# Where the last two slots of the input projection are computed in a two-block decoder kernel

## The reference

```
for l in range(2):
    h = x @ w_in[l]                  # gla: q k v g lr | rwkv: r k v w a g | nsa: q kc vc ks vs kw vw gate
    o_gla  = gla_mixer(q, k, v, g, lr)              # chunked decayed linear attention
    o_rwkv = rwkv7_mixer(token_shift(r, k, v, w, a, g))   # delta rule, solved by chunks of 128
    o_nsa  = nsa_mixer(rope(q, kc, ks, kw), vc, vs, vw, gate)   # compressed, selected, windowed
    x = layer_norm(ALPHA * x + concat(o_gla, o_rwkv, o_nsa) @ w_out[l])
    x = layer_norm(ALPHA * x + (silu(x @ gate[l]) * (x @ up[l])) @ down[l])
x = second_block(x)                  # attention and recurrence, then the experts
```

## Time and profile before

| | us |
|---|---|
| median of 3 runs | 2019.58 |
| lowest, highest | 2018.89, 2026.96 |
| the profiled execution | 2023.03 |
| its span, first to last instruction | 2021.2 |
| layer 0: first projection product to first output product | 10.94 to 220.90 |
| TensorE busy | 1966.1 (97%) |
| VectorE busy | 855.1 (42%) |
| ScalarE busy | 313.4 (16%) |
| mean granted TensorE clock | 0.993 |

### The profile page before, as it was taken

The page is one execution under the profiler, slowest core; times in us unless marked ns, Lnnn a source line. Parts: engine busy times, 40 slices in busy tenths (PEclk is TensorE's granted clock), DMA queues, the critical chain, the costliest instruction groups (busy, mean ns, idle before and its releaser), DMA issues.

```text
span 2021.2 us, 24513 instructions
## 1 busy us (share of the span) xinstructions
PE 1966.1 (97%) x9835; PEld 1115.1 (55%) x9835; DVE 855.1 (42%) x1538; ACT 313.4 (16%) x725; POOL 45.1 (2%) x62
## 2 busy tenths in 40 slices
PE   8999999999999999999999999999999999999997
PEld 7878588748777588749553333333333333333332
DVE  1487588865587586754731111111111111111112
ACT  1335211101435111103410000000000000000001
POOL 0021000000021000000000000000000000000000
PEclk9999999999999999999999999999999999999999
DMA  8540067646630165436298999999999999999996
GB/s 332 217 158 1 32 234 308 251 167 278 263 126 1 41 226 199 171 154 266 89 393 373 428 429 429 427 429 429 427 430 427 430 429 427 429 427 430 429 428 287
DMA packets 44275, 598.75 MB, mean 296 GB/s; under 512 B 5056, under 2 KB 5360, under 8 KB 8464
## 3 DMA queue, kind: packets, MB, share of 16 engines
q1 hardware_dynamic: 44208, 597.82, 71.9%
HBM read 596.73 MB, written 1.07 MB: 296 GB/s over the span
## 4 chain that ended last, share of the span: by engine, by line
PE 82%; DMA 15%; DVE 3%; issue 0%; ACT 0%; SPq 0%; DVEq 0%
PE ps L2349 18%; DMA ring<-in_stream 15%; PE ps L1404 12%; PE ps L2397 8%; PE ps L1489 7%; PE ps L402 6%; PE ps L2323 3%; PE ps L1273 3%; PE ps L361 2%; PE ps L2338 2%; PE ps L419 2%; PE ps L2434 2%; PE ps L1820 1%; PE ps L1986 1%; PE ps L1150 1%; PE ps L1167 1%
## 5 line engine op out<-in xcount | busy, mean ns | idle before, releaser
L2349 PE MATMUL ps<-ring,HT 128*64 128x512 f32 x2176 | 479.4, 594 | 20.0 <-DMA ring<-in_stream 19.2
L2349 PEld LDWEIGHTS ps<-ring,HT 128*64 128x64 f32 x2176 | 152.9, 137 | 340.1 <-issue 289.3
L2397 PE MATMUL ps<-SB,HT 128*64 128x512 f32 x1088 | 249.2, 612 | 0.9 <-ACT HT L2460 0.9
L2505 DVE TENSOR_SCALAR HT<-ps 128x512 f32<-128x512 f32 x34 | 23.5, 692 | 449.8 <-PE ps L2349 449.8
L2397 PEld LDWEIGHTS ps<-SB,HT 128*64 128x64 f32 x1088 | 77.0, 140 | 170.2 <-issue 170.2
L1404 PE MATMUL ps<-ring,SB 128*128 128x256 f32 x704 | 156.0, 379 | 0.3 <-DVE SB L331 0.3
L2454 ACT ACTIVATE HT<-HT 128x512 f32<-128x512 f32 x34 | 21.5, 631 | 843.9 <-DVE HT L2505 843.9
L1404 PEld LDWEIGHTS ps<-ring,SB 128*128 128x128 f32 x704 | 133.6, 190 | 18.8 <-issue 0.7
L2517 DVE TENSOR_TENSOR HT<-ps,TOK 128x512 f32<-128x512 f32 x34 | 23.5, 692 | 281.3 <-PE ps L2397 281.3
L402 PE MATMUL ps<-SB,ring 128*128 128x256 f32 x576 | 126.9, 384 | 1.3 <-DMA ring<-in_stream 1.3
L402 PEld LDWEIGHTS ps<-SB,ring 128*128 128x128 f32 x576 | 110.8, 193 | 17.1 <-issue 1.6
(11 more groups left out here) (489 smaller groups left out, 2251.8 us busy)
## 6 DMA issues: line engine op xcount, KB each, us to landing
ring<-in_stream SPq DMA_DIRECT2D x210, 2048.0 KB, 16.6
SB<-in_stream SPq DMA_DIRECT2D x68, 2048.0 KB, 24.8
SB<-in_ln SPq DMA_DIRECT2D x8, 512.0 KB, 7.0
CST<-in_const SPq DMA_DIRECT2D x1, 1362.0 KB, 5.5
PAR<-in_layer SPq DMA_DIRECT2D x2, 558.5 KB, 11.6
X<-in_x SPq DMA_DIRECT2D x1, 1024.0 KB, 4.9
HN<-in_head_norm SPq DMA_DIRECT2D x2, 512.0 KB, 12.8
SB<-in_cond_row SPq DMA_DIRECT2D x2, 512.0 KB, 10.9
```

Of the source, the lines that this page charges most:

```text
L2349: m = pe.matmul(ps[HD * half:HD * (half + 1), a, :], XE[:, 2 * b + k, q * SLOTS_E:(q + 1) * SLOTS_E], w[:, k, a, half, :], start=False, st ...
L2397: m = pe.matmul(ps[HD * c:HD * (c + 1), 3, :], EHT[:, k, HD * b:HD * (b + 1)], w[:, k, c, :], start=b + k == 0, stop=b + k == 4, skip_grou ...
```

## The change

It does these things, in both layers alike.

- TensorE runs group 9 behind `rwkv_ranks_pe`, so that the gate and rank products follow group 8.
- Rotary pieces 0 and 1 are turned right behind group 9, and VectorE finishes them within `gla_decay_dve`, ahead of its wait for ScalarE's decay.
- The 24 gate columns become a group of their own (11): 16 products of 24 columns, ahead of the rows of `TOK`. Rows of tile 0 (now group 12) come behind it, ahead of the mixers.
- Rows of tile 1 (now group 13) are computed within score units 2 to 6, in pieces of 1, 1, 2, 2 and 2 products of 512 columns. The unread products of all eight units are gone. The compression's hidden products now wait until that group has been copied.
- The value columns (now group 14, 16 products of 256 columns) are computed in steps 2 and 3, at the places of the unread products: 4, 4 + 2, 2 and then 4, the last behind the scores of step 3. The six unread products of step 3 are gone, and a wait for the copy of group 14 stands there.
- ScalarE copies groups 10 and 11 behind its query and ahead of its root, 12 where 13 was, 13 behind the last key, and 14 in step 3 between a copy of the inverse and the exponentials of attention unit 1.
- The blocks of the compression move to another part of SBUF, and GpSimd starts on them at `rw_ops`, not at the end of the projection. Slot 5 is released by group 14, slot 6 by group 13.

```
-                return "proj_ready", 15 * l + [2, 4, 6, 8, 10, 13, 15][s]
+                return "proj_ready", 15 * l + [2, 4, 6, 8, 10, 15, 14][s]
...
+        def project_gates_pe(pe, l):
+            w = slot(AT["in", l, 5]).rearrange("p (k n) -> p k n", k=KT)
+            pe.wait_ge(S("proj_evac"), 15 * l + 8)
+            pe.wait_ge(S("rope"), ROPE_PIECES * l + 2)
+            for t in range(NT):
+                for k in range(KT):
+                    m = pe.matmul(ps[:, proj_bank(11), 24 * t:24 * (t + 1)], XT[:, k, t * P:(t + 1) * P], w[:, k, 384:408],
+                                  start=k == 0, stop=k == KT - 1)
+            m.then_inc(S("proj_ready"), 1)
...
+            for k in ks:
+                m = pe.matmul(ps[:, proj_bank(12 + t), :], XT[:, k, t * P:(t + 1) * P], w[:, k, 0:512],
+                              start=k == 0, stop=k == KT - 1)
...
+                m = pe.matmul(ps[:, proj_bank(14), t * 256:(t + 1) * 256], XT[:, k, t * P:(t + 1) * P], w[:, k, P:P + 256],
+                              start=k == 0, stop=k == KT - 1)
...
             ins.then_inc(S("gla_zb"), 1)
+            rope_dve(v, l, 0, I, L)
+            rope_dve(v, l, 1, I, L)
             v.wait_ge(S("gla_zb"), l + 1)
...
-            pool.wait_ge(S("proj_ready"), 15 * (l + 1))
+            pool.wait_ge(S("rw_ops"), l + 1)
...
+        TOKEN_PIECES = (range(0, 1), range(1, 2), range(2, 4), range(4, 6), range(6, 8))
...
                 if u + 2 < ROPE_PIECES:
                     rope_pe(pe, l, u + 2)
-                    clock_pe(pe, 0, 384, P, 4)
-                else:
-                    pe.wait_ge(S("rope"), ROPE_PIECES * l + 3)
-                    clock_pe(pe, 7, 0, 256, 1)
+                elif u < 7:
+                    project_tokens_pe(pe, l, 1, TOKEN_PIECES[u - 2])
...
                 if s == GLA_BACK:
-                    clock_pe(pe, 3, 0, 256, 3)
+                    project_values_pe(pe, l, 0, range(4))
...
+                if s == GLA_BACK + 1:
+                    project_values_pe(pe, l, 1, range(4, 8))
...
                 if s == GLA_BACK:
-                    clock_pe(pe, 3, 0, 256, 3)
+                    project_values_pe(pe, l, 0, range(4, 8))
+                    project_values_pe(pe, l, 1, range(2))
                     back_pe(pe, 2 * l, G_XC, 4)
-                    clock_pe(pe, 3, 0, 256, 3)
+                    project_values_pe(pe, l, 1, range(2, 4))
...
                     if u == 1:
-                        clock_pe(pe, 3, 0, 256, 6)
+                        pe.wait_ge(S("proj_evac"), 15 * (l + 1))
                         pe.wait_ge(S("cmp_kv"), l + 1)
...
+            project_act(act, l, (13,))
             inverse_product_act(act, l, FIRST_HALF)
...
+                if u == 1:
+                    project_act(act, l, (14,))
...
-                    project_pe(pe, l, range(5))
+                    project_pe(pe, l, range(9))
...
                 gla_gate_pe(pe, l)
                 rwkv_ranks_pe(pe, l)
-                project_pe(pe, l, (5,))
+                project_pe(pe, l, (9,))
+                for p in range(2):
+                    rope_pe(pe, l, p)
                 rwkv_norm_pe(pe, l)
-                project_pe(pe, l, (6,))
+                project_pe(pe, l, (10,))
+                project_gates_pe(pe, l)
+                project_tokens_pe(pe, l, 0, range(KT))
                 rwkv_bonus_pe(pe, l)
                 mixers_pe(pe, l)
...
                 project_act(act, l, (9,))
                 gla_decay_act(act, l, L)
                 rwkv_gates_act(act, l, I)
-                project_act(act, l, (10,))
                 gla_query_act(act, l)
-                project_act(act, l, (11, 12))
+                project_act(act, l, (10, 11))
                 rwkv_decay_act(act, l, I)
                 rwkv_values_act(act, l)
-                project_act(act, l, (13,))
+                project_act(act, l, (12,))
                 gla_key_act(act, l, 0)
                 gla_key_act(act, l, 1)
-                project_act(act, l, (14,))
                 mixers_act(act, l)
```

More of the change, by code:

```diff
@@ L383, in project_first_pe, with project_pe @@
                     m.then_inc(S("proj_ready"), 1)
-        def project_pe(pe, l, slots):
-            def bank_free(g):
-                if g >= 13:
+        def project_pe(pe, l, groups):
+            for g in groups:
+                need_slot(pe, AT["in", l, g // 2])
+                w = slot(AT["in", l, g // 2]).rearrange("p (k n) -> p k n", k=KT)
+                if g >= 4:
+                    pe.wait_ge(S("proj_evac"), 15 * l + g - 3)
+                if g == 10:
+                    pe.wait_ge(S("rope"), ROPE_PIECES * l + 2)
+                for j in range(2 if g < 10 else 1):
+                    for k in range(KT):
+                        m = pe.matmul(ps[:, proj_bank(g), j * T:(j + 1) * T],
+                                      w[:, k, (2 * (g % 2) + j) * P:(2 * (g % 2) + j + 1) * P],
+                                      XT[:, k, :], start=k == 0, stop=k == KT - 1)
+                m.then_inc(S("proj_ready"), 1)
@@ L389, in bank_free, with project_tokens_pe @@
+        def project_tokens_pe(pe, l, t, ks):
+            w = slot(AT["in", l, 6]).rearrange("p (k n) -> p k n", k=KT)
+            if ks[0] == 0:
+                need_slot(pe, AT["in", l, 6])
+                if t == 0:
                     pe.wait_ge(S("gla_zb"), l + 1)
                     pe.wait_ge(S("rw_gates"), l + 1)
[L391 to L421, removed]
@@ L430, in project_act @@
                     to, n = HT[:, 20, :], T
-                elif g < 13:
-                    to, n = NV[:, g - 11, :], 280
-                else:
-                    to, n = TOK[:, g - 13, :], 512
-                nc.scalar.activation(to, ps[:, proj_bank(g), 0:n], ACT.Copy,
+                elif g == 11:
+                    to, n = NV[:, :, 256:280], 48
+                elif g < 14:
+                    to, n = TOK[:, g - 12, :], 512
+                else:
+                    to, n = NV[:, :, 0:256], 512
+                come = ps[:, proj_bank(g), 0:n]
+                if g in (11, 14):
+                    come = come.rearrange("p (t c) -> p t c", t=NT)
+                nc.scalar.activation(to, come, ACT.Copy,
                                      scale=HD ** -0.5 if g == 0 else 1.0).then_inc(S("proj_evac"), 1)
@@ L1040, in cmp_hidden_pe @@
                 pe.wait_ge(S("cmp_blocks"), 18 * (l + 1))
+                pe.wait_ge(S("proj_evac"), 15 * l + 14)
             w = []
```

33 lines of the change are left out of this document (20 added, 13 removed).

## The result

The changed kernel takes 2067.18 us (median of 4, 2060.55 to 2070.88), the kernel before in the same comparison 2019.24 (median of 4): ratio 1.0226, 95% interval 1.0185 to 1.0267. It is slower, as forecast, but by 47.9 us and not by 26.4, and lies above the range. The profiled execution took 2060.55, span 2058.7, so it is the shortest of the four; the mean granted clock of the others was 0.974 to 0.976, its own 0.978.

What follows compares the result with a forecast made beforehand. It took TensorE's nearly unbroken row of work through each layer as the bound. Terms 4.4 + 8.2 + 2 x 2.5 + 2 x 1.4 + 6.0 = 26.4 us on the median 2019.58 gave 2046.0, range 2032 to 2057.

Steps and rivals of the forecast that it cites:

- The bill of TensorE's work: TensorE per layer: 10.9 us removed, values 0.4 less, gate columns 3.6 added; 7.7 us won if only its work counted.
- The units: Eight score units, first pair products to hidden products: added rows less removed unread products, 2.5 us longer in each layer.
- The steps: Steps 2 and 3: value products in place of unread ones, 1.4 us longer in each layer, between 0 and 2.7.
- ScalarE's copies hold the decay and the root: Ahead of the mixers: group copies delay ScalarE's decay and root, first pair products 4.4 us later in layer 0, 8.2 in layer 1.
- The sum without the clock: Both layers: delays ahead of the mixers, units and steps together, without TensorE's clock falling, 20.4 us.
- clock term: TensorE at half speed behind new waits: 2.0 us in each layer plus one of three doubtful waits, 6.0, between 0 and 12.
- the clock falls at many places: Rival: half speed in the first units and the ranks too, four losses of 2 us more, 2054 us; chance 0.10.
- The queues of the loads: SyncE's list: slot 5 released some 70 us later, four loads behind it; price nothing, worst case 8 us in a layer.
- The rival of TensorE's own work: Removed unread products decide at the front: some 3 to 7.7 us won a layer, 2004 to 2013 us; chance 0.09.

Runs made afterwards that it cites:

- e2_fill: Changed kernel with unread products of 256 columns put into TensorE's four waits ahead of the mixers, every order left as is: 2041.9 us, ratio 1.0119 to the kernel before.
- e1_copy9: Changed kernel with ScalarE copying group 9 behind the rwkv gates, not ahead of the decay: 2063.1 us, ratio 1.0219 to the kernel before.
- e8_fill_ranks: Changed kernel with 4 and 7 unread products in the waits ahead of the rank products of layers 0 and 1: 2060.92 us, ratio 1.0198 to the kernel before.
- e7_fill_bonus: Changed kernel with 7 unread products in the wait ahead of the bonus transposes: 2056.93 us, ratio 1.0212 to the kernel before.
- e10_keys: Changed kernel, copies of groups 9 to 12 and rotary pieces moved later, gate products 128 columns wide, unread products ahead of ranks and in units 0, 1: 2015.06 us.
- e5_free: Changed kernel with ScalarE copying groups 9 to 11 behind root and exponentials, rotary pieces turned behind gate columns and finished behind first keys: 2055.94 us.
- e3_group9_back: Changed kernel with TensorE running group 9 ahead of the gate products again: 2046.78 us, ratio 1.0135 to the kernel before.
- e4_before_thin_units: Kernel before without the four unread products of 128 columns in each of score units 0 and 1: 2020.77 us, ratio 1.0032 to the kernel before.

## Why the prediction was right in kind and wrong in size

- *The bill of TensorE's work.* Right. The gate columns were put at 3.6 and took 3.50. The units became 3.4 us longer at full clock (forecast 2.5); in e2_fill TensorE waits 0.94 us for VectorE ahead of the second pair products, which is about the difference. The steps became 1.3 and 1.4 longer (forecast 1.4).
- *ScalarE's copies hold the decay and the root.* Right in effect. At full clock the pair products came 3.9 and 8.9 us later (forecast 4.4 and 8.2). It was incomplete as a cause, as e1_copy9 showed: VectorE's rotary pieces held the same chain at the same time. In layer 0 the decay was 8.3 us late and not 5.5, which is the clock again: the rank products and group 9 ran partly at half speed.
- *The sum without the clock.* Forecast 20.4; e2_fill, in which the clock held but for some 3 us in layer 1, is 22.9 above the kernel before.
- ***The step that failed is the clock term***: "6.0, between 0 and 12". By the medians of changed kernel and e2_fill it is 2067.2 - 2041.9 = 25.3 us, four times the value taken and twice the upper bound; by their profiled executions it is 21.4, of which the table places 17.7. The price of a fall was taken from the first products of the kernel, 1.8 us, and the number of falls as three. Both were too small: 17.7 over five falls is 3.5 each. It fell in or behind five waits of this profile: ahead of the ranks and ahead of the norm product in both layers, and ahead of the bonus in layer 0. I had called the first of these, in layer 0, nothing, because 2.2 us seemed short; the measured wait was 1.96. And half speed lasted from 80 to 87, 98 to 107 and 124 to 137 us, where the pattern I priced from had lasted 4. Last, the delay was on the path each time, as the table shows: 4.7 us ahead of the mixers and 5.1 in the units in layer 0, 7.9 ahead of them in layer 1. In other executions layer 1's units fell too, as e8_fill_ranks shows with 8.4 us.
- *The rival "the clock falls at many places"* came nearest. It had the ranks and the first units among the places; at 2 us a fall its time was 2054, 13 us short, and its chance 0.10. Its condition, units that start thinly without unread products, is not what decides: e2_fill and e7_fill_bonus have no unread products in the units and ran them at full clock. In these traces it was the wait ahead of the bonus: open in e8_fill_ranks the clock fell in both layers, filled in e7_fill_bonus in none.
- *A reading that was wrong.* The prediction says that the trace before shows no fall between 11 us and the last product. It holds for the two layers. In the second block the clock was low six times between 1073 and 1978 us, with TensorE busy:

```profile
1076.00:1080.00 4.00, 4.00 (x14) 1.91 (x11) 0.00 (x0) 0.38 (x1) 0.00 (x0) 0.50 0.99 426
```

- *The queues of the loads*: the price of nothing stood. The stretch from the hidden products to the output product grew by the 1.3 of the steps alone.
- *The rival of TensorE's own work.* With the holds taken out (e10_keys) the sign does change, but the win is 3.9 us over both layers and not 3 to 7.7 in each, and e10_keys has the unread products ahead of the ranks besides.

The Trainium skill (TensorE: Matmul & The Clock Gate, "HAM oscillation") has it that each burst after a wait starts at the low clock. The trace agrees with this in five of the six waits of the changed kernel's two layers, and not in the sixth, the 3.26 us ahead of layer 1's bonus. The same page ("What's actually happening") puts the penalty of the climb to full clock, for modelling, at under 1% of a typical kernel's span. The 1.8 us that the prediction read at the start of this kernel are 0.1% of it; the falls together cost 25.3 of 2067 us, 1.2%.

## What to carry to other kernels

When work is moved ahead of or behind others on one engine, list for every other engine what stands ahead of the critical chain in its program, and look for a second and a third hold: taking one out of a series may win nothing, as in e1_copy9. Unread products put into the waits tell in one run what part of a loss is clock and what part order. A wait of TensorE that is hidden by slack was not free here where thinly filled work followed it.

## What the runs showed of the hardware that I had not expected

- Behind a wait of 1.96 us of TensorE, which had been fully busy before, the granted clock went to 0.50 within 2 us of its return, and stayed for 7 us of full activity. In all four kernels that leave the waits ahead of the ranks open with group 9 behind them (1.96 us in layer 0; the changed kernel, e1_copy9, e5_free, e7_fill_bonus) it fell there in both layers. In the other ten, where these waits are filled or absent, it fell there in 2 of 20 places (layer 1 of e3_group9_back and of e4_before_thin_units), for 3.4 us each, with TensorE busy.
- The same sequence of products ran 21.2 us at full clock when it was entered at full clock, and 29.6 us in e8_fill_ranks when it was entered behind a wait of 3.3 us. Behind the same wait in the changed kernel it took 26.3 in layer 0 and 21.2 in layer 1.
- Sixteen products of 24 columns on 128x128 weights in a row, without a gap, were followed by a fall of the clock in 6 of 16 rows (0.56 in the stretch at the end of one); the same with 128 columns took about as long (3.73 and 3.65 us) and kept it at 1.00 in six of six rows, and so did the narrow ones mixed with products of 512 columns.
